# Seven-product block multiplication for the conv output projection and for the C and x projections of the second sequence half

## What is computed

```python
u = rms_norm(h, g_pre)
c_b, c_c, c_x, c_z, q, k, v, r, lr_f, lr_b, m_a, m_b = split(u @ w_in)   # 8 blocks of 1024, some smaller
y_conv = c_b * short_conv_centred(c_c * c_x, conv_w) * silu(c_z)         # "C" is c_c, "x" is c_x, "B" is c_b
p_conv = y_conv @ w_out_c                                                # the conv output, "oc"
y_gla  = rms_norm(o_forward + o_backward) * silu(r)                      # chunked gated linear attention
p_gla  = y_gla @ w_out_g                                                 # "og"
merged = sigmoid(m_a) * p_conv + sigmoid(m_b) * p_gla
out    = h + rms_norm(merged @ w_out, g_post)
```

## Time and profile before

| | us |
|---|---|
| three runs of the kernel, median (lowest to highest) | 2921.14 (2919.9 to 3465.07) |
| the profiled execution, its own time | 2921.19 |
| span of its slowest core (core 3) | 2919.6 |
| spans of the 8 cores | 2909.6 to 2919.6 |
| granted clock of the cores, mean | 0.995 to 0.997 |

### The profile page before, as it was taken

One profiled execution on the slowest core, in us unless ns is written; L12 is line 12 of the kernel. 1 busy time (PEld: TensorE's weight loads), 2 busy tenths in 40 slices (PEclk: granted clock), 3 DMA queues, 4 the chain that ended last, 5 costly groups with the idle time before them and its releaser, 6 DMA issues.

```text
span 2919.6 us, 53947 instructions; the slowest of 8 cores (2909.6 to 2919.6 us)
## 1 busy us (share of the span) xinstructions
PE 2851.8 (98%) x16092; PEld 1468.0 (50%) x16092; DVE 1815.4 (62%) x2786; ACT 1381.3 (47%) x2567; POOL 831.7 (28%) x1278
## 2 busy tenths in 40 slices
PE   6999999999999999999999999999999999999998
PEld 3565644444456554444456555444445655544443
DVE  4766662564677776465476677556457777745554
ACT  5766651232456764232256686323235767522222
POOL 3343333331323223232242312223123222321212
PEclk9999999999999999999999999999999999999999
DMA  7786548853633334374373323447356322354334
GB/s 183 134 140 116 125 101 183 232 173 113 197 106 77 75 84 115 110 232 127 111 216 81 75 68 89 123 142 230 97 152 170 78 72 71 84 137 127 118 112 140
DMA packets 340764, 373.44 MB, mean 128 GB/s; under 512 B 208112, under 2 KB 218352, under 8 KB 339968
## 3 DMA queue, kind: packets, MB, share of 16 engines
q1 hardware_dynamic: 326944, 344.61, 41.8%
q0 software_dynamic: 13536, 25.37, 6.0%
HBM read 287.69 MB, written 63.50 MB: 120 GB/s over the span
## 4 chain that ended last, share of the span: by engine, by line
PE 94%; DMA 2%; DVE 1%; issue 1%; POOL 1%; ACT 0%; SPq 0%; DVEq 0%; POOLq 0%; ACTq 0%
PE ps L479 94%; DMA sb_onT<-x 0%; DMA sb_onT<-sb_ON 0%; DMA wsc<-sb_W 0%; DMA sb_W<-w_all 0%; DMA sb_KT<-sb_GR 0%; POOL sb_stat L674 0%; PE ps L484 0%; POOL sb_SB L514 0%; DMA sb_ycT<-x 0%; DVE sb_CS L509 0%; DVE sb_ycT L505 0%; DVE sb_TB L509 0%; POOL sb_stat L514 0%; DVE sb_CS L505 0%
## 5 line engine op out<-in xcount | busy, mean ns | idle before, releaser
L479 PE MATMUL ps<-sb_uT,sb_W 128*128 128x512 bf16 (+2 forms) x7840 | 1625.9, 366 | 1.9 <-DMA sb_W<-w_all 1.2
L479 PEld LDWEIGHTS ps<-sb_uT,sb_W 128*128 128x128 bf16 (+1 forms) x7840 | 707.8, 98 | 808.9 <-issue 20.4
L496 ACT ACTIVATE sb_CS<-ps 128x512 f32<-128x512 f32 (+2 forms) x528 | 281.2, 540 | 636.2 <-PE ps L479 605.2
L505 DVE TENSOR_TENSOR sb_CS<-ps,sb_CS 128x512 f32<-128x512 f32 (+1 forms) x408 | 281.0, 691 | 187.9 <-PE ps L479 177.6
L509 DVE SCALAR_TENSOR_TENSOR sb_CS<-sb_CS,ps 128x512 f32<-128x512 f32 x256 | 175.8, 687 | 295.6 <-PE ps L479 284.3
L505 POOL TENSOR_TENSOR sb_GR<-sb_CS 128x512 bf16<-128x512 f32 x128 | 162.1, 1267 | 671.0 <-DVE sb_CS L509 658.5
L479 PE MATMUL ps<-sb_GR 128*128 128x512 bf16 (+2 forms) x1792 | 347.5, 318 | 1.1 <-POOL sb_GR L505 1.1
L505 POOL TENSOR_TENSOR sb_CS<-sb_CS 128x512 f32<-128x512 f32 x128 | 164.8, 1291 | 276.7 <-DVE sb_CS L509 168.6
L479 PE MATMUL ps<-sb_V,sb_uT 128*128 128x256 bf16 x2048 | 239.3, 274 | 0.0
L479 PE MATMUL ps<-sb_onT,sb_W 128*128 128x512 bf16 x1024 | 232.2, 379 | 2.6 <-DVE sb_onT L509 2.6
L509 DVE SCALAR_TENSOR_TENSOR sb_CS<-sb_CS,sb_convw 128x512 f32<-128x512 bf16 x256 | 209.8, 832 | 39.8 <-ACT sb_CS L496 27.6
(11 more groups left out here) (125 smaller groups left out, 2888.7 us busy)
## 6 DMA issues: line engine op xcount, KB each, us to landing
sb_W<-wsc SPq DMA_DIRECT2D x440, 256.0 KB, 2.6
sb_onT<-x SPq DMA_DIRECT2D x56, 512.0 KB, 5.4
sb_W<-wst SPq DMA_DIRECT2D x112, 256.0 KB, 2.8
sb_W<-w_all POOLq DMA_DIRECT2D x80, 256.0 KB, 6.2
sb_GR<-x SPq DMA_DIRECT2D x40, 512.0 KB, 5.5
wsc<-sb_W SPq DMA_DIRECT2D x80, 256.0 KB, 4.4
y<-sb_GR SPq DMA_DIRECT2D x32, 512.0 KB, 3.4
sb_ycT<-x SPq DMA_DIRECT2D x32, 512.0 KB, 5.4
```

The lines of the kernel that those rows point to most:

```text
L479: S.add("pe", lambda e: e.matmul(out, lhsT=lhsT, rhs=rhs, start=start, stop=stop, skip_group_check=more), r, w, cost=max(0.025, free_n(rhs ...
L496: S.add("act", lambda e: e.activation(out=out, in_=in_, func=func, **kw), r, w, table=TABLE.get(func), cost=0.17 + 0.82e-3 * free_n(in_) + ...
L505: S.add(eng, lambda e: e.tensor_tensor(out=out, in0=a, in1=b, op=op), r, w, cost=ecost(eng, free_n(out), narrow(out, a, b)))
```

## The change

`class Seven` is made general (which activations, which sums, which weight pool) and used for the conv output too: the pair is (oc d, oc d+1), so the blocks d go in pairs. Its activation sums `TY` (four, of y_conv, in `GR` 32 to 48 KB) are built by `ysums` on the DVE at the end of the conv. Its results are multiplied by `finy`. A second class, `SevenA`, does C and x of the features 2 to 7 of the second half from the same `TT` sums that the gates of that half use; z and B stay plain units and stand between. Its sums of weights are built once, in the first half of the first sequence (`pair_sums`). The buffers for tanh become four instead of two (new region `G2`), `W1` gets five buffers instead of three, the space for that is taken from a scratch area for POOL's transfers, and the merges become a chain of their own.

```diff
-    nc = bass.Bass("TRN2", target_bir_lowering=False)
+    nc = bass.Bass("TRN2", target_bir_lowering=False, dynamic_dma_scratch_size=4096)
...
-        w1 = WPool("W1", [Buf("W1", i * 2048, 2048) for i in range(3)])
+        w1 = WPool("W1", [Buf("W1", i * 2048, 2048) for i in range(5)])
...
+        sdA = [Buf("G2", i * 2048, 2048) for i in range(3)]
+        TY = [Buf("GR", 32 * KB + i * 4096, 4096) for i in range(4)]
...
+            def done(f, bk):
+                if f == 0:
+                    o_ap, o_k = ccb[0](F32)
+                    act(o_ap, bk[0][:, 0:512], AF.Copy, bk[1], o_k)
+                else:
+                    o_ap, o_k = pv(BF16, 1, 512)
+                    c_ap, c_k = ccb[0](F32)
+                    tt("dve", o_ap, bk[0][:, 0:512], c_ap, ALU.mult, bk[1] + c_k, o_k)
+
+            def total(f, bk, part):
+                s_ap, s_k = part(F32)
+                o_ap, o_k = ccb[1](F32) if f == 0 else (s_ap, s_k)
+                tt("dve", o_ap, bk[0][:, 0:512], s_ap, ALU.add, bk[1] + s_k, o_k)
+                if f:
+                    c_ap, c_k = ccb[1](F32)
+                    p_ap, p_k = pv(BF16, 513, 512)
+                    tt("pool", p_ap, o_ap, c_ap, ALU.mult, o_k + c_k, p_k)
...
+        def ysum(hh, bf, part):
...
+            tt("dve", o[0], x[0], y[0], ALU.subtract, x[1] + y[1], o[1])
...
+            for n in range(len(pairs)):
+                put("SW", lambda n=n: load(n), None, [("qm", 0, 3, 1, 1), ("mb", 0, 0, n, 0)] + ([("SW", n - 2)] if n > 1 else []))
+                put("SX", lambda n=n: sums_b(*fetch[n % 2], pairs[n][0], tmp), ("SW", n), [("ma", 0, 0, n + 1, 1)])
...
+        class SevenA:
...
+            def keep(self, name, z):
+                bk = G["sA", name]
+                o_ap, o_k = sdA[z](F32)
+                act(o_ap, bk[0][:, 0:512], AF.Copy, bk[1], o_k)
...
+            def p6(self):
+                b_ = G["sA", "b"] = nps(True)
+                self.mul(b_, 1, 512, self.tt(1), True)
+                s_ap, s_k = sdA[0](F32)
+                tt("dve", b_[0][:, 0:512], b_[0][:, 0:512], s_ap, ALU.add, b_[1] + s_k, b_[1])
+
+            def p5(self):
+                e = G["sA", "e"] = nps(True)
+                self.mul(e, 1, 0, self.tt(0), True)
+                self.keep("e", 2)
+                self.keep("b", 1)
+                rel(self.h[1])
...
+            def finy(d, f, s, bk, s_=None):
+                a_ap, a_k = ta[f * 2 + s](F32)
+                if s_ is None:
+                    stt(a_ap, a_ap, 1.0, bk[0][:, 0:512], ALU.add, ALU.mult, bk[1] + a_k, a_k)
+                    return
+                s_ap, s_k = s_(F32)
+                tt("dve", s_ap, bk[0][:, 0:512], s_ap, ALU.add, bk[1] + s_k, s_k)
+                stt(a_ap, a_ap, 1.0, s_ap, ALU.add, ALU.mult, s_k + a_k, a_k)
...
+                    ysums(b, 1, [("cb", (b, 1, 7), 1), ("st", b, 0, 7)])
...
-                    order = ["p1", "p5", "p6", "p2", "p3", "p7", ("oc", 0), "p4", ("oc", 1), ("og", 0), ("og", 1)]
...
+                six = ["p1", "p5", "p6", "p2", "p3", "p7"]
+                for o in ([(0, p) for p in six] + [("og", 0, 1), (0, "p4")] + [(1, p) for p in six] + [("og", 0, 0), (1, "p4")] +
+                          [(2, p) for p in six] + [("og", 1, 1), (2, "p4"), ("og", 1, 0)]):
...
-                eng = min(("pool", "dve"), key=lambda e: max(S.free[e], S.free["pe"]) + ecost(e, 1024, False))
-                tt(eng, yv, yv, xv, ALU.add, yk + xk, yk)
+                tt("dve", yv, yv, xv, ALU.add, yk + xk, yk)
...
-                units = ca + cz + cbb
...
+                for u in [ca["p1"], ca["p6"], ca["p5"], ca["p2"], pend[0], ca["p3"], ca["p7"], pend[1] or t7.pop(0), ca["p4"], cz[0],
+                          t7.pop(0) if j in (3, 5) and t7 else None, cz[1], t7.pop(0) if t7 else None]:
```

261 lines of the change are left out of this document (189 added, 72 removed).

## The result

| | before | after |
|---|---|---|
| three or more runs, median, us | 2921.14 | 2961.33 |
| runs, lowest, us | 2919.9 | 2956.64 |
| profiled execution: time, span of its slowest core, us | 2921.19, 2919.6 | 2956.64, 2955.1 |
| granted clock of the cores | 0.995 to 0.997 | 0.989 to 0.994 |

The ratio of the times is 1.0134, 95% interval 1.0091 to 1.0178: the changed kernel is 1.3% **slower**. I had forecast 1.1% faster, 2889 us; the measured time is outside the range, on the other side. (Some executions of nearly every version had one or both halves of the chip at a lower clock and took longer; they are left out of all ratios and lowest times here.)

The account below looks back on a forecast made before the run. PE bounds the kernel, busy 2851.8 of 2919.6 us. Span 2919.6 - 44.7 + 13 + 2 + 2 - 2 - 2 = 2887.9 us, plus 1.6 gives 2889.5, predicted as 2889 us; range 2872 to 2907.

Parts of the forecast that it names:

- Removed: Conv output and C and x: 208 matmuls fewer at 0.2147 us each, saving 44.7 us.
- First: Start of second half's gates: `TY` subtractions delay p3 and p4; 3.3 us, 4 times, 13 us, bounds 0 and 20.
- Second: Start of second half's conv: p1's copy waits for POOL's last merge; 0.5 us, 4 times, 2 us, bounds 0 and 5.
- the 22 us by which I had DVE too low: DVE busy time over the whole kernel: from 1815 to about 1990 us, 69% of the new span, not the bound.
- Third: p7 within the conv, 24 times, waits for sum and copy; 0.1 us each, 2 us, bounds 0 and 10.
- Fourth: Transfers in first sequence's first half: -4 us from deeper buffers, +2 crowding; -2 us, bounds -4 and +12.
- The end: Last residuals and stores: last residual but one moves to DVE, last store is alone; -2 us, bounds -4 and 0.
- Bound by transfers: Rival: first half of first sequence, weights come late, PE waits 11 us more; 2900.5 us, chance 0.13.
- Slower than before: Rival: hand-overs at p3 and p7 of oc sets cost 1.1 us a set; 12.5 us slower, 2933 us, chance 0.04.

Follow-up runs that it names:

- 14: Like 13, but C and x by seven products in the last sequence only; lowest 2926.7 us, ratio 1.0031.
- 16: Change, first sequence plain, sums moved, late `TY`, mended og, five `W1` buffers after first gates, C and x by seven in last sequence alone; 2900.35 us, ratio 0.9933.
- 13: Change with first sequence plain, sums from SBUF blocks, late `TY`, mended og, last transpose ahead of 2 MB load; seven products from second sequence; 2926.52 us, ratio 1.0018.
- 17: Like 16, but C and x by seven products from the second sequence on; lowest 2902.22 us, ratio 0.9941.
- run 7: The kernel before with the small scratch area and five `W1` buffers instead of three; lowest 2928.68 us, ratio 1.0033.
- run 18: The change with three `W1` buffers until the end of the first gates, five after; lowest 2959.64 us, ratio 1.0138.
- run 10: The change with og after the second gate set in a first half's first block, earlier positions' og first in the last pair; 2948.26 us, ratio 1.0096.
- run 12: The change with output-weight load, first store of weight sums and fetches for C and x sums behind the last transpose; lowest 2968.45 us, ratio 1.0161.
- the fastest version: The kernel of 16; lowest 2900.35 us, ratio 0.9933.
- run 2: The change with C and x by seven products only from the second sequence on, sums built as in the change; lowest 2947.74 us, ratio 1.0103.

## Why the prediction was wrong

- **Removed, right.** 208 matmuls, at 0.2158 us each by the starts (I had 0.2147): 44.9 us.
- **First, right.** I forecast 2.6 us for p3 and 1.1 for p4; the trace of core 2 has 2.30 in all four sequences and 0.52 in two. The later `TY` sums gave back 8.8 us of my 13. The four stages lost 17.6 us in all (the 13.8 of 64 matmuls not gained, and 3.8); the rest is in part the stops before p4 of the oc pairs, below.
- **Second, too small.** The start of the conv waits 1.27 us for the copy in each of sequences 2 to 4, not 0.5. The merge itself takes 1.27 us, as I had it. What stands ahead of it doesn't; DVE and POOL of the change in order of time, core 2:

```profile
2705.69 1.27 POOL L505 TENSOR_TENSOR sb_GR<-sb_G 128x512 bf16<-128x512 f32 x1 [1.29 <-DVE sb_G L509]
2706.25 1.25 DVE L509 SCALAR_TENSOR_TENSOR sb_G<-sb_G,sb_CS 128x512 f32<-128x512 f32 x1
...
2708.25 1.26 POOL L505 TENSOR_TENSOR sb_GR<-sb_G 128x512 bf16<-128x512 f32 x1 [1.29 <-DVE sb_G L509]
```

  The new multiply of `finy`, both inputs in SBUF, starts within a merge and ends 0.54 us after that merge's end; the same operation with an input from PSUM takes 0.68 us in all. By form, count, busy, mean ns:

```profile
L509 DVE SCALAR_TENSOR_TENSOR sb_G<-sb_G,sb_CS 128x512 f32<-128x512 f32 x56 | 69.6, 1243 | 6.5 <-DVE sb_CS L505 0.9
L509 DVE SCALAR_TENSOR_TENSOR sb_G<-sb_G,ps 128x512 f32<-128x512 f32 x72 | 48.5, 677 | 18.0 <-PE ps L479 18.0
```

  So the rule of the Trainium skill ("SBUF — State Buffer", "Who interferes with whom": the later of two such instructions waits for the whole of the earlier) holds here, and 0.7 us later, as I had worked out by it, is what came; but it is DVE that is held, and the merge is late by that. By it the term was 5 us, by my rows 2; measured 1.4 us with the restart, three times. It also more than covers the 22 us by which I had DVE too low: 56 x 0.57 = 32 us. Missed beside it: a short stop before p4 of each oc pair, 0.2 us, four times a half, some 6 us over seven halves.
- **Third, wrong where a next sequence is prepared.** In the last conv it holds: nothing is lost beside the start's wait. In sequences 2 and 3 the change lost 4.6 and 6.5 us. Seven products gained nothing or 1 us there over the plain ones, shown by runs 14 and 16 against 13 and 17. I had counted DVE's share of the stage (73%) and one feature's order; the next sequence's input was in neither.
- **Fourth, the step that failed.** "I take -4 for these and +2 for the crowding": measured +14.4 us up to the end of the first gates and, with the 5.2 us not gained, +22.9 in the conv behind. So this term, -2 with an upper bound of 12, was 37. Three things were wrong. The deeper buffers, which I had as a gain, are a loss of 8.5 us by themselves (run 7). Some 4 us of it stand already before the first og unit, in the attention ahead, where the order of the matmuls changes too; what makes them was not looked into. Then the planner starts the gates 19 matmuls earlier, their stores and write-backs go ahead of the last transpose in SP's queue, and the first og unit comes another 7 us later, of which some 4 come back, as the two waits for weights are gone. Up to matmul 3000 the change follows run 7 (7.2 and 7.0 us behind before); the other 6 to 7 us of its first gates come in the last 188 matmuls, as waits for weights. The buffers are the cause in run 7 and can't be called the only one in the change, where three buffers cured nothing (run 18). The stores of the oc sums, 4 times 2 with the same two buffers as the gate sums, I had not priced at all. And I took the rush to end at 550 us: it runs into the conv. There DVE, in order, stops for a buffer whose store is on its way, and PE waits for the `TT` sums that are queued behind. The chain of waits of the change, core 3:

```profile
544.13 8.02 DMA wst<-sb_CS
...
557.55 10.19 PE ps L479 x36
```

PE there, in order of time:

```profile
557.55 3.57 PE L479 MATMUL ps<-sb_AT,sb_W 128*128 128x512 bf16 x8 [6.50 <-DVE sb_AT L505]
```

- **Not in the prediction at all: the order of og and the merges.** The new loop puts og of block 0 behind 24 matmuls of the gates instead of 44, before the last head's output is there (2.3 to 3.3 us a time on core 2, three times), and the merge that the first output tile needs at the very end (6.0 us in all). Both stood in the diff; run 10 gave back some 8 us (1.3 a time at the first, 3.6 in all at the second).
- **The end** was right in sign: -4.8 us behind the last matmul.
- **The rivals.** "Bound by transfers" had the right place and less than a third of the size (11 us more than my forecast, where 39 came). "Slower than before" had the right sign and the wrong place: the hand-overs within an oc set cost 0.2 us, as I had counted against it; 78 us over 52 sets are 1.5 us each, but half of that is the first sequence.

## What to carry to other kernels

A gain of a fraction of a microsecond in each of fifty sets is eaten by a dozen waits of 1 to 7 us, so before the saving is summed, every place where the new order puts a consumer earlier than before must be checked against its producer, in the diff, one by one. Set-up work that runs once (weight sums, write-backs) belongs where the queue is idle and from blocks that are there anyway; with the first sequence left plain, that work moved, the orders mended and the buffers made deeper only afterwards, the scheme was 0.6 to 0.7% faster (runs 16 and 17) instead of 1.3% slower. And this scheduler, given more buffers, didn't only prefetch: it moved everything behind them forward, and stores with it. Nor was a wait behind a large copy cured by reordering alone: with the 2 MB copy behind the transpose, the next weights came late instead (runs 12 and 13).

## What the runs showed of the hardware

- A transpose by DMA behind a copy of 2 MB on the same queue took 11.2 us from issue to landing in the kernel before (core 3, issued at 425.28, the copy at 424.05) and 10.31 us in the change (432.12, with 3.5 MB of copies in the 4 us ahead of it); with the copy behind it, in run 12, it took 2.4 us, as did those issued from 404 to 424 us in the kernel before, in the median.
- A stop of 3.41 us of PE was followed by about 15 matmuls at the lower clock, so it cost 6.6 us. One of 2.30 us was followed by 3.4 us of it in two of four places on the same core.
- The mean granted clock fell from 0.996 to 0.990 in the change and is 0.996 to 0.998 in the fastest version. On core 2 of the change, between 420 us and the last matmul, nine of the ten stretches at the lower level (3.4 or 6.8 us each) begin within 3 us of the end of a stop of 1.9 us or more.
- In run 12 a third level shows: 0.81 for some 150 us on cores 0, 1, 6 and 7, from 464 us on, while cores 3 and 5, with a stop at the same place, show only the two levels of 1.2 and 2.4 GHz. Cores 0 and 1 of run 2 have it too, for 161 us from 528 us on.
- A DVE multiply of two SBUF inputs beside a POOL merge takes 1.24 us on average instead of 0.68.
